# Second block of a fused two-block transformer kernel: its early part in groups of tiles 0-1, 2 and 3, its conv FFN for tiles 0-2 and then tile 3

## The reference, cut to what matters

```python
z = rms_norm(x, mix_norm_g) @ w_in                # q, k, v, gates, zg, zc
y_nsa  = nsa_mixer(...)                           # 8 heads, compressed, selected and window branches
y_gmlp = gmlp_mixer(zg, ...)
y_conv = conformer_conv_mixer(zc, ...)            # causal depthwise convolution, 31 taps
x = x + concat(norms of the three) @ w_out
x = x + memory_cross_attention(x, mem, ...)       # wq, wk, wv, wo of 1024x1024
h = causal_depthwise_conv(rms_norm(x, g) @ w_up)  # w_up 1024x5632, 3 taps
x = x + (silu(gate) * up) @ w_down                # w_down 2816x1024
```

## Time and profile before

| | us |
|---|---|
| median of 3 runs | 2905.69 (2903.39 to 2906.92) |
| the profiled execution | 2902.87 |
| its span in the profile | 2901.1 |
| PE busy | 2408.7 (83%) |
| DVE busy | 1765.4 (61%) |
| ACT busy | 1124.4 (39%) |
| POOL busy | 665.2 (23%) |
| moved by DMA | 838.74 MB, 289 GB/s in the mean |

### The profile page before, as it was taken

How to read it: one execution, slowest core, us unless ns; L and a number is a source line. 1 busy time by engine, 2 the same in 40 slices (tenths; PEclk the granted TensorE clock), 3 DMA queues, 4 the chain that set the end, 5 groups by cost and what they waited for, 6 DMA issues and landing times.

```text
span 2901.1 us, 31007 instructions
## 1 busy us (share of the span) xinstructions
PE 2408.7 (83%) x10834; PEld 1655.5 (57%) x10834; DVE 1765.4 (61%) x4230; ACT 1124.4 (39%) x2762; POOL 665.2 (23%) x569
## 2 busy tenths in 40 slices
PE   8999999879978649778958588577984799988998
PEld 7786666657744327536626434354762376655873
DVE  2101311598797778676999898888998417312430
ACT  2101311242533764354442578464554225412210
POOL 0000000122343344332233334443234102100000
PEclk9999999989989879999979566699996699999999
DMA  6555343589999999999889989999999653443443
GB/s 205 173 153 166 96 145 126 213 333 371 403 412 417 416 392 391 419 398 393 314 333 416 368 324 379 390 419 419 416 418 419 258 161 111 152 131 94 153 153 116
DMA packets 160972, 838.74 MB, mean 289 GB/s; under 512 B 17400, under 2 KB 21896, under 8 KB 95024
## 3 DMA queue, kind: packets, MB, share of 16 engines
q0 software_dynamic: 73728, 536.90, 45.8%
q1 hardware_dynamic: 82464, 287.75, 28.6%
q10 hardware_dynamic: 4624, 12.11, 1.2%
HBM read 828.27 MB, written 8.41 MB: 288 GB/s over the span
## 4 chain that ended last, share of the span: by engine, by line
PE 50%; DVE 22%; ACT 13%; DMA 10%; issue 4%; POOL 0%; ACTq 0%; DVEq 0%; SPq 0%
PE ps L909 24%; DMA BIG<-in_uv,BIG 9%; DVE BIG L1951 6%; PE ps L929 5%; DVE X L1928 5%; PE ps L930 5%; PE ps L1153 5%; PE ps L910 3%; ACT L1446 2%; PE ps L1180 2%; DVE BIG L1859 1%; DVE BIG L1856 1%; PE ps L1123 1%; PE ps L1102 1%; ACT WK L1228 1%
## 5 line engine op out<-in xcount | busy, mean ns | idle before, releaser
L2168 POOL DMA_INDIRECT BIG<-in_uv,BIG x512 | 622.0, 1215 | 1635.1 <-DVE X L1928 576.0
L909 PE MATMUL ps<-BIG,RING 128*128 128x256 f32 x3472 | 810.6, 386 | 15.2 <-DMA RING<-in_w_cq 4.9
L909 PEld LDWEIGHTS ps<-BIG,RING 128*128 128x128 f32 x3472 | 665.5, 193 | 148.0 <-issue 26.5
L1951 DVE CUSTOM_DVE_ANT_0 BIG<-BIG 128x1024 f32<-128x1024 f32 x512 | 619.2, 1217 | 87.1 <-DMA BIG<-in_uv,BIG 84.8
L1928 DVE SCALAR_TENSOR_TENSOR X<-BIG,small,X 128x1024 f32<-128x1024 f32 x333 | 426.3, 1280 | 75.0 <-ACT small L1450 74.3
L1446 ACT ACTIVATE small<-small 128x1 f32<-128x1 f32 x512 | 102.7, 201 | 640.5 <-DVE small L1951 636.3
L909 PE MATMUL ps<-WK,RING 128*128 128x256 f32 x1232 | 291.0, 389 | 21.3 <-DVE BIG L1707 19.3
L909 PEld LDWEIGHTS ps<-WK,RING 128*128 128x128 f32 x1232 | 238.6, 195 | 62.2 <-DVE BIG L1707 26.8
L929 PE MATMUL ps<-RING,BIG 128*128 128x512 f32 (+1 forms) x448 | 225.7, 585 | 5.6 <-DVE BIG L1686 2.4
L930 PE MATMUL ps<-RING,BIG 128*128 128x512 f32 (+1 forms) x448 | 223.5, 580 | 0.0
L1279 ACT ACTIVATE BIG<-ps 128x256 f32<-128x256 f32 (+2 forms) x143 | 56.5, 397 | 375.8 <-PE ps L910 316.7
(11 more groups left out here) (258 smaller groups left out, 2860.1 us busy)
## 6 DMA issues: line engine op xcount, KB each, us to landing
RING<-in_w_up SPq DMA_DIRECT2D x88, 512.0 KB
RING<-in_w_down SPq DMA_DIRECT2D x66, 512.0 KB
RING<-in_w_pq SPq DMA_DIRECT2D x32, 512.0 KB
RING<-in_w_cc SPq DMA_DIRECT2D x16, 512.0 KB
RING<-in_w_cx SPq DMA_DIRECT2D x16, 512.0 KB
RING<-in_w_cb SPq DMA_DIRECT2D x16, 512.0 KB
RING<-in_w_cv SPq DMA_DIRECT2D x16, 512.0 KB
RING<-in_w_gc SPq DMA_DIRECT2D x16, 512.0 KB
```

What stands on the lines that cost most here:

```text
L909: e.matmul(ps[:, 0:256], W[:, j, :], src[:, j, 0:256], start=j == 0, stop=False)
L1951: e.tensor_tensor_reduce(out=u, in0=HF[:, t % 2, :], in1=u, scale=1.0, scalar=0.0, op0=ALU.mult, op1=ALU.add, accum_out=dots[:, k % 8:k % ...
L2168: e.indirect_dma_start(out=slot[i], out_offset=None, in_=I["uv"], in_offset=bass.IndirectOffsetOnAxis(ap=IDX[:, t, c:c + 1], axis=0)).then ...
```

## The change

`EARLY = ((0, 1), (2,), (3,))` and `LATE = ((0, 1, 2), (3,))` are the new groups: everything up to and with the cross attention runs for tiles 0-1, then tile 2, then tile 3; the conv FFN for tiles 0-2 and then tile 3. In the weave stand now `second(0)`, `second(1)` (tile 2) and `ffn(0)` (up projection of three tiles, 384 wide); after the weave `end()` runs `second(2)` (tile 3) with the down chunks of tiles 0 to 2 beside it (66, one tile each), `ffn(1)` (up projection for tile 3, 128 wide) and its 22 down chunks. For a group of one tile the NSA phase has 12 steps with 8 units, each step with twice as many taps of the convolution at half the width, and cross attention has 8 steps with 4 units. The planned cost of each step and of a row is as before. The row slots stay at seven from the scores of tiles 2 and 3 on, since the last five pieces of the wider FFN buffer lie in the eighth.

```diff
+EARLY = ((0, 1), (2,), (3,))
+LATE = ((0, 1, 2), (3,))
...
-        if i >= (8 if self.lent_from is None or (3, 3) in self.chosen else 7):
+        if i >= (8 if self.lent_from is None else 7):
...
     def late_down(self):
-        for i in range(2):
+        for i in LATE[0]:
             for f in range(22):
...
+        if nt == 1:
+            other = {1: ("gmlp_norm", h, 0), 3: ("gmlp", h, 0), 8: ("conv_out", h, 0), 10: ("y_sq", h, 1), 11: ("y_sq", h, 2)}
-        for step in self.phase(True, ((8.0, "nsa", h, i) for i in range(20))):
+        for step in self.phase(True, ((8.0, "nsa", h, i) for i in range(8 * nt + 4))):
...
-            yield from beside(1 + step[3] % 2)
+            yield from beside(2 + step[3] % 2)
...
+    def end(self):
+        rest = self.late_down()
...
+        yield from self.second(2, False, beside)
+        yield from self.ffn(1, False, beside)
+        for f in range(22):
+            k = self.next_ring()
+            yield 0, "chunk", "down", f, k
+            yield 3.4, "down", 1, f, k, (0,)
+        yield 0, "mark", ("out", 1)
+        yield from self.last(1)
...
         yield from self.second(0, True)
+        while ("total", 2) not in self.reached or (3, 3) not in self.chosen:
+            self.light = True
+            yield "wait"
+        self.light = False
+        yield from self.second(1, True)
+        yield from self.ffn(0, True)
         self.light = True
...
-        yield from (s[1:] for s in self.second(1, False))
+        yield from (s[1:] for s in self.end())
...
+        HTu = [WKF[:, 0:3072].rearrange("p (a b) -> p a b", a=8), WKF[:, 0:1024].rearrange("p (a b) -> p a b", a=8)]
+        UPT = [[WKF[:, 3072 + 384 * i:3456 + 384 * i] for i in range(2)], [WKF[:, 2048 + 512 * i:2176 + 512 * i] for i in range(4)]]
+        AF = [[at_(L0 + 384 * f if f < 17 else SLOT0 + 14336 + 384 * (f - 17), 384) for f in range(22)],
+              [at_(L[2] + 128 * f, 128) for f in range(22)]]
...
         def conv_ops(h, i):
             ops = [(m, s) for s in range(31) for m in range(2)]
-            return ops[4 * i:4 * i + 4]
+            n = 8 // NT[h]
+            return ops[n * i:n * i + n]
 
         def cmp_n(h):
-            return (0, 15) if h == 0 else (15, 31)
+            return ((0, 15), (15, 23), (23, 31))[h]
...
+                n = 128 * len(tiles_of(site, h))
                 for j in range(7):
-                    e.matmul(ps[:, 0:256], W[:, j, :], src[:, j, 0:256], start=j == 0, stop=False)
+                    e.matmul(ps[:, 0:n], W[:, j, :], src[:, j, 0:n], start=j == 0, stop=False)
```

More of the change, by code:

```diff
@@ L258, in cross_rest @@
         yield 0, "mark", ("xs", layer, h)
-        yield from self.phase(True, ((4.0, "cross", layer, h, i, lean) for i in range(12)))
+        n = 2 if layer == 1 else len(EARLY[h])
+        for step in self.phase(True, ((4.0, "cross", layer, h, i, lean) for i in range(4 * n + 4))):
+            yield step
+            yield from beside(1)
         yield from self.proj_tok("co" if layer == 1 else "xo", h, 2, lean)
@@ L325, in late_down, with second @@
         yield (0, "mark", ("out", 0)),
[L327 to L332, removed]
+    def second(self, h, lean, beside=lambda n: ()):
+        nt = len(EARLY[h])
         yield 0, "mark", ("s2", h)
@@ L376, in second @@
         yield 0, "y_scale", h
-        yield from beside(7)
+        yield from beside(8)
         for k in range(8):
@@ L381, in second, with ffn @@
         yield from self.proj_tok("ou", h, 2, lean)
[L382 to L395, removed]
+        yield from self.cross(2, h, lean, beside)
+    def ffn(self, f, lean, beside=lambda n: ()):
+        yield 0, "mark", ("f", f)
+        yield from self.norm_steps(("ffn2", f), lean)
+        yield from beside(100)
+        for k in range(8):
+            yield (3.0 if k == 7 else 0), "trans", ("ffn2", f), k, lean
+        self.norming = False
+        yield 0, "mark", ("up", f)
+        for step in self.proj_T("up", f, 11, lean):
+            yield step
+            if f and step[1:] == ("out_T", "up", f, 1, 3, lean):
+                yield from self.last(0)
     def last(self, h):
@@ L400, in last, with beside @@
         yield 0, "store", h
+    def end(self):
+        rest = self.late_down()
+        def beside(n):
+            for steps in islice(rest, n):
+                yield from steps
+        yield from self.second(2, False, beside)
[6 more added lines that the diff above has]
+        yield from self.last(1)
     def first_a(self):
@@ L611, in program @@
-        TMPz = WKF[:, 1024:3072].rearrange("p (a b) -> p a b", a=2)
[L612 to L619, removed]
+        L = [L0, L0, SLOT0 + 8448]
@@ L1092, in nsa @@
                 u = i - 4
[L1093 removed]
+                if 0 <= u < len(units):
                     qb, r, g = units[u]
@@ L1247, in norm_out @@
                 o = n["o"]
-                if not n["pool"]:
-                    own()
-                    e.activation(n["tmp"][:, 0, :], n["src"][:, 0, :], ACT.Copy, scale=small[:, o:o + 1]).then_inc(
-                        act.sem, act("nrm", key, 0))
+                own()
+                for i in range(0, len(key_tiles(key)), 2):
+                    e.activation(n["tmp"][:, i, :], n["src"][:, i, :], ACT.Copy, scale=small[:, o + i:o + i + 1]).then_inc(
+                        act.sem, act("nrm", key, i))
             def trans(key, k, lean):
```

345 lines of the change are left out of this document (193 added, 152 removed).

## The result

The kernel after takes 3001.25 us (median of 4 runs, 2999.9 to 3002.36) against 2906.31 (4 runs, 2903.39 to 2914.76) for the kernel before: a ratio of 1.0328, 95% interval 1.0316 to 1.0341, 95 us slower. The forecast was 2984. The profiled execution has a span of 2998.4 us, and the sum of the prediction's terms was a span of 2979. So 19 us are to be found.

The account below looks back on a forecast made before the run. Bytes (DVE in tiles 0-1's NSA) bound the kernel while rows run, PE the tail. Rows to 2295, plus 55.5, 238.5 and 390, gave a span of 2979 us, forecast 2984 against the median; range 2945 to 3035.

Parts of the forecast that it names:

- Where the rows end: In the weave, the 91 rows still following at 2000 us were to end at 2295, bounds 2268 and 2320.
- The three pieces: Last rows of the weave: 43 with projection and cmp chunks 136 us, 38 with NSA 122, 10 with ou chunks 37.
- What is left of the weave: After the last row, all in the open on PE: 55.5 us up to xo, then 238.5 for `ffn(0)`.
- The first rival: One-tile passes in the open do not hide their weight load: 89 us more, 3073, or half way 3028; chance 0.08.
- The term of 79: Up projection of tile 3 in the tail: 44 chunks at 1.79 us, 79 us.
- the cover of `last(0)`: In tile 3's up stage, `last(0)` hides in PE's eight banks; without that cover it costs 9 us.
- "PE waiting for RING in the last up stage": Sign of being wrong, in tile 3's up stage; the weights were costed at nothing, with 293 GB/s needed.
- The other signs: Wrong if the first NSA stretch has a DMA share under 0.9; right if tile 3's NSA steps take near 9 us.
- the second rival: Seven slots starve the rows: both NSA phases lose a seventh, 26 + 18 us, 3028; chance 0.08.
- Work ahead of the rows: Rival: idle PE beside the last 91 rows gets some 80 us further on, so 2904, no loss; chance 0.06.
- Clock, and two readings: In the earlier trace's tail, granted clock is 0.95 to 1.00 in busy stretches; PE is always busy except in norms.
- The top of the range: Upper end of the forecast time, 3035, set by the slots and half of the unhidden load.

Follow-up runs that it names:

- all sums moved to PE: Kernel with both cures, but all row sums of the light phases (DA, NSA, cross attention) on TensorE instead of two of three: 2853.79 us.
- the late store: Kernel after, with the store of tiles 0-2 issued only behind the last up chunk: 2985.42 us.
- the seven-slot run: Kernel before, with seven row slots to the last row once the eighth is lent: 2909.09 us, ratio 1.0002.
- the pace runs: Rows planned at 3.2 us (tile 2) and 3.9 (tile 3) instead of 2.5: on the kernel after 2921.83 us, on the kernel before 2950.08.
- the prices: Kernel after with rows at 3.2 and 3.9 us and weight chunks priced by width (1.8, 5.2, 3.4 us): 2876.48 us.
- the two kernels with all light sums on PE: Both cures with all light-phase row sums on TensorE, 2853.79 us; the same with more rows planned beside the three-tile up stage, 2852.00 us.
- both cures: Kernel after with rows at 3.2 and 3.9 us, chunk prices by width, and the store of tiles 0-2 behind the last up chunk: 2857.41 us.

## Why the prediction was right, and the 17 us that it missed

The mechanism and nearly every term hold: the up projection in the open sets the loss, and one term, taken at nothing, makes nearly all of what is missing. The measured lengths are from the windows above, or from further cuts of the same trace.

| term | predicted us | measured us |
|---|---|---|
| 43 rows beside projections and cmp | 136 | 140 |
| rows beside tile 2's NSA | 122 (38 rows) | 113 (36 rows) |
| last rows beside ou | 37 (10 rows) | 42 (14 rows) |
| last row | 2295 | last dot 2291.3 |
| tile 2 up to and with xo | 55.5 | 55 |
| norm of three tiles | 11.5 | 14 |
| up, three tiles | 227 | 227.3 |
| first norms, projections, cmp of tile 3 | 59.8 | 59.0 |
| NSA of tile 3 with 30 down chunks | 100 | 94.7 |
| y with eight chunks | 16 | 20.1 |
| ou to ffn's norm | 89 | 89.5 |
| up, one tile | 79 | 97.2 |
| down, then last norm and store | 46 | 46.7 |

- **Where the rows end.** Right to 4 us. The three pieces miss by +4, -9 and +5 and cancel, which is luck in part: the last had 14 rows where 10 were planned. (Its sum is a little off too: 10 rows and 10 chunks are 15.7 MB, not 15.4.) In the middle one DVE was busy 100.39 of 113 us, 0.89, where 0.90 was taken. That share was right, but all sums moved to PE gave hardly a gain, so it is a share that this mix reaches and not DVE's limit.
- **What is left of the weave.** The price scaled to 384 columns (5.16 a chunk) was exact: 44 chunks in 227.28.
- **One-tile passes.** The first rival (the weight load shows) fell: chunks start 1.79 us apart, sixteen passes of 0.112. In the window 2900 to 2950 PE and PEld are both busy in 50.00 of 50 us and nothing shows of the load; the 155 ns estimated in that rival did not come. The term of 79 was itself right: with the store out of the way the stage took 80.76.
- **The step that failed** is the cover of `last(0)`: "`last(0)` hides in PE's eight banks; without that cover it costs 9." Its work on DVE and ACT does hide. Its store does not: it is queued on SyncE ahead of the ring's loads and waits there for DVE. It was a term of nothing and measured 18 (97.2 for 79): 15.59 of idle, and 2.9 the restart, whose first two chunks took 3.76 and 2.69 us for 1.79 (granted clock 0.50 over the first). By the late store it is 16 of the time. The other terms cancel to about 1, which makes the 19 of the span. Against the medians it is 17, since the forecast had added 2.8 for the place of the profiled execution under its median and this one (3000.24) lies 1.0 under. I had counted the queue past which the ring's bytes flow (293 GB/s needed, 294 measured) and not the queue in which they are asked for. "PE waiting for RING in the last up stage" was on the prediction's own list of signs of being wrong, and it came, for another reason than the bytes.
- **The other signs.** The first NSA stretch kept a DMA share of 0.91, next to the 0.9 below which it would have spoken against the forecast. The NSA steps of tile 3 took 7.9 us each (94.7 in 12), for the 9 named.
- **Slots.** Nothing, as taken; the second rival fell with the seven-slot run, as far as that goes (old grouping).
- **Work ahead of the rows.** It did not happen by itself: the last dot fell with tile 2 within its ou, as the list had it. At the end of tile 2's NSA 14 rows were left where the list has 9: a lead of five rows, as the prediction had read from the kernel before. But the rival's point, that the loss turns on where rows and work stand to each other, is what the pace runs confirm. Its deciding point was 78 us; moving the rows by the list alone gave 79 back and came to 15 us above the kernel before, and the prices took it past.
- **Clock, and two readings.** Granted clock is not "0.95 to 1.00 in each busy tail stretch": in the earlier trace rows the cmp stretch (PE busy 10.63 of 11.40 us) has 0.75 and the one from 2290.0 has 0.84. It cost the forecast nothing, since cmp was taken over as measured (11.3 us at 0.74 in the kernel after). Nor is PE busy all the time in each stage but the norms: in cross attention it is for 17.77 of 23.10 us. The top of the range, 3035, covers the price of the slots or half of the unhidden load, 44 us each, and not both.

The Trainium skill, "Trainium Kernel Development and Optimization", section "Key Constraints", says that DMAs started from several engines share the same 16 DMA engines, and that issuing from several saves only the time of issue. In this trace the time of issue is small, 0.33 us of the chain for line 900, but a load also inherits the wait of what is ahead of it in its queue, 17.2 us here. No run here moved the store to another engine's queue.

The large loss itself is that of the prediction: the up projection, 152 us in the open before, is 227 + 97 now. What the runs add is that this was no property of the grouping. It came from leaving the planned pace (2.5 us a row) as it was, so that the rows ran out some 70 us before the stage with the most PE time for each byte began. With 56 rows placed beside that stage it costs the same 227 us, and the rows have moved out of the time before it.

## What to carry to other kernels

When a list or a planner fixes the order of in-order queues, a regrouping must be costed again with it: put the work that is bound by bytes beside the stage with the most engine time for each byte, and price steps by their new width. When a step is moved, follow each of its instructions into its own queue, the DMA-issuing one too, and ask how long the head of that queue waits and how long the buffer behind it (here six ring entries, 11 us) lasts. A store goes behind the loads that the next stage needs. And stop adding cover when another engine's queue is full: here DVE at 146.61 of 150 us, where what was won ahead of the stage came back as a wait behind it.

## What the runs showed of the hardware

- A stream of 128x128 float32 weight loads and 128-column matmuls ran at 0.112 us a pass with both PE and PEld busy in all of the time. At this width the load was still hidden.
- A three-tile float32 projection at full clock was not slowed by 58.7 MB of gathered rows beside it, with the DMA share at 0.89, nor at 1.01 (PE 150.00 of 150 us).
- The granted clock from 1634 to 1818 us was 0.76 and 0.79 in the two kernels with all light sums on PE (702 and 697 matmul records), and 0.60 to 0.68 in nine other kernels of this document (564 to 626 records). PE's busy time hardly differs: 133.70 us of 184 with both cures, 135.76 with all sums on PE.
